# A two-block transformer kernel: nine norms take their inverse root as a square root on ACT and a reciprocal on DVE

## What is computed

```python
def rmsnorm(x, g):
    x32 = x.astype(jnp.float32)
    y = x32 * lax.rsqrt(jnp.mean(x32 * x32, axis=-1, keepdims=True) + EPS)
    return (y * g.astype(jnp.float32)).astype(x.dtype)
...
    x = x + gt1 * (jnp.concatenate([conv_x, attn_x, gla_x], axis=-1) @ w_out)
    x = x + gt2 * swiglu(rmsnorm(x, g2) * (1 + sc2) + sh2, w_up, w_down)
...
        h = rmsnorm_2(x, norm_mix_w[l])
        x = x + hybrid_mixer(h, w_in[l], ...)
        h = rmsnorm_2(x, norm_xattn_w[l])
        x = x + memory_cross_attention(h, mem_n, w_q, w_kv, w_o)
        h = rmsnorm_2(x, norm_ffn_w[l])
        x = x + swiglu_2(h, ...)      # layer 0; a mixture of 8 experts in layer 1
```

## Time and profile before

| | us |
|---|---|
| median of 3 runs | 2685.38 |
| lowest, highest | 2685.04, 2687.94 |
| profiled execution: its own time | 2687.88 |
| profiled execution: its span | 2686.0 |

### The profile page before, as it was taken

How to read it: one execution, slowest core, us unless ns; L and a number is a source line. 1 busy time by engine, 2 the same in 40 slices (tenths; PEclk the granted TensorE clock), 3 DMA queues, 4 the chain that set the end, 5 groups by cost and what they waited for, 6 DMA issues and landing times.

```text
span 2686.0 us, 42788 instructions
## 1 busy us (share of the span) xinstructions
PE 2511.2 (93%) x17242; PEld 2223.3 (83%) x17242; DVE 1757.4 (65%) x2364; ACT 1475.3 (55%) x1888; POOL 27.9 (1%) x85
## 2 busy tenths in 40 slices
PE   4998799999999889999889999897999999999998
PEld 2876579999997689988789998686888888888886
DVE  3445856455455765556555546556888988988887
ACT  3235544444443655455554435554777777777776
POOL 0000000000000000000000001000000000000000
PEclk7998999999999989999999999898999999999999
DMA  7224525445442635445134545231899999999995
GB/s 281 104 100 158 189 95 188 180 182 188 177 160 90 254 136 181 180 159 176 61 126 157 185 177 174 79 136 69 331 358 350 351 357 352 350 356 352 351 356 222
DMA packets 81593, 565.98 MB, mean 211 GB/s; under 512 B 9280, under 2 KB 12608, under 8 KB 13568
## 3 DMA queue, kind: packets, MB, share of 16 engines
q1 hardware_dynamic: 80112, 559.95, 56.1%
q0 software_dynamic: 1296, 3.38, 0.5%
HBM read 559.92 MB, written 1.05 MB: 209 GB/s over the span
## 4 chain that ended last, share of the span: by engine, by line
PE 85%; DVE 8%; ACT 4%; issue 2%; DMA 0%; SPq 0%; DVEq 0%; ACTq 0%
PE psum L232 83%; DVE ring_lo L226 2%; ACT ring_hi L223 1%; DVE hT L739 1%; PE psum L662 1%; PE psum L1880 1%; DVE hT L429 1%; ACT hT L703 1%; DVE hT L1242 1%; ACT Z L711 0%; DMA ring<-in_stream 0%; ACT L415 0%; DVE h_lo L439 0%; DVE Z L1216 0%; DVE Z L1215 0%
## 5 line engine op out<-in xcount | busy, mean ns | idle before, releaser
L226 DVE TENSOR_TENSOR ring_lo<-ring,ring_hi 128x2048 fp32r<-128x2048 f32 x479 | 1096.8, 2291 | 458.5 <-ACT ring_hi L223 455.4
L223 ACT ACTIVATE ring_hi<-ring 128x2048 fp32r<-128x2048 f32 x479 | 916.1, 1914 | 376.9 <-PE psum L232 375.6
L232 PE MATMUL psum<-a_hi,ring_hi 128*128 128x256 f32 (+1 forms) x2448 | 732.7, 299 | 59.8 <-DVE h_lo L437 20.0
L232 PE MATMUL psum<-a_hi,ring_lo 128*128 128x256 f32 (+1 forms) x2448 | 727.3, 297 | 0.0
L232 PE MATMUL psum<-h_lo,ring_hi 128*128 128x256 f32 (+1 forms) x2128 | 629.0, 296 | 0.0
L232 PEld LDWEIGHTS psum<-a_hi,ring_hi 128*128 128x128 f32 x2448 | 476.6, 195 | 78.6 <-issue 43.9
L232 PE MATMUL psum<-ring_hi,a_hi 128*128 128x512 f32 (+1 forms) x1680 | 521.0, 378 | 5.9 <-DVE h_lo L437 3.7
L232 PEld LDWEIGHTS psum<-a_hi,ring_lo 128*128 128x128 f32 x2448 | 476.1, 194 | 10.5
L232 PEld LDWEIGHTS psum<-h_lo,ring_hi 128*128 128x128 f32 x2128 | 414.2, 195 | 7.6
L232 PEld LDWEIGHTS psum<-ring_hi,a_hi 128*128 128x128 f32 x1680 | 313.5, 189 | 58.1 <-issue 4.1
L232 PE MATMUL psum<-ring_lo,a_hi 128*128 128x512 f32 (+1 forms) x976 | 353.2, 362 | 0.0
(11 more groups left out here) (261 smaller groups left out, 2373.5 us busy)
## 6 DMA issues: line engine op xcount, KB each, us to landing
ring<-in_stream SPq DMA_DIRECT2D x529, 1024.0 KB, 4.9
mixT<-mixT POOLq DMA_DIRECT2D x32, 71.0 KB, 5.8
cst<-in_constants SPq DMA_DIRECT2D x1, 1216.0 KB, 15.0
xT<-in_xT SPq DMA_DIRECT2D x1, 1024.0 KB, 9.7
xT<-in_ctxT SPq DMA_DIRECT2D x1, 1024.0 KB, 11.9
xT<-in_memT POOLq DMA_DIRECT2D x1, 1024.0 KB, 6.0
out_y<-hT SPq DMA_DIRECT2D x2, 512.0 KB, 3.1
Z<-in_level_masks SPq DMA_DIRECT2D x1, 448.0 KB, 15.3
```

What stands on the lines that cost most here:

```text
L223: e.activation(hi, raw, ACT.Copy).then_inc(sem("piece_rounded"), 1)
L226: e.tensor_tensor(lo, raw, hi.bitcast(F32), ALU.subtract).then_inc(sem("piece_split"), 1)
L232: ins = pe.matmul(*args, **kw)
```

## The change

`act_rms` computes one function, the square root, and gives its semaphore a new name, `rms`. DVE, which had waited for `inverse_rms`, now calls `dve_invert`: it waits for `rms`, takes the reciprocal in place, waits for its own instruction to finish and goes on. Two preloads name the set of the square root in place of that of the logarithm; the one at the end of the third feed-forward run (`run == 2`), after which `act_two_norms` follows, keeps the logarithm's set.

```diff
@@ -394,7 +394,7 @@
         def act_square_residual(n):
             def step(act, g):
                 if g == 0:
-                    act.preload_act_table_set("natural_log")
+                    act.preload_act_table_set("sqrt_and_others")
@@ -411,8 +411,12 @@
         def act_rms(act, b, n0, n1):
             await_next(act, "mean_square")
             rs = mixT[:, 0, n0:n1]
-            link(act, act.activation(rs, bank[b][:, n0:n1], ACT.Ln, bias=EPS))
-            act.activation(rs, rs, ACT.Exp, scale=-0.5).then_inc(sem("inverse_rms"), 1)
+            act.activation(rs, bank[b][:, n0:n1], ACT.Sqrt, bias=EPS).then_inc(sem("rms"), 1)
+
+        def dve_invert(dve, n0, n1):
+            await_next(dve, "rms")
+            rs = mixT[:, 0, n0:n1]
+            link(dve, dve.reciprocal(rs, rs))
@@ -571,7 +575,7 @@
-            act.preload_act_table_set("natural_log")
+            act.preload_act_table_set("natural_log" if run == 2 else "sqrt_and_others")
@@ -2286,7 +2290,7 @@
                 if layer == 0:
                     dve_first(dve)
-                await_next(dve, "inverse_rms")
+                dve_invert(dve, 0, 2 * T)
```

More of the change, by code:

```diff
@@ L2309, in _ @@
                               at=OUT_BANKS)
-                await_next(dve, "inverse_rms")
+                dve_invert(dve, 0, n)
                 dve_apply(dve, [b1_segment(layer, 1, 0)])
@@ L2325, in _ @@
                 else:
-                    await_next(dve, "inverse_rms")
+                    dve_invert(dve, 0, T)
                     dve_apply(dve, [b2_segment("norm_mix", 1)])
```

## The result

The changed kernel takes 2699.6 us (median of 4 runs, 2699.1 to 2706.0) beside 2685.2 for the kernel before (4 runs, 2684.1 to 2687.9): a ratio of 1.0055 with a 95% interval of 1.0043 to 1.0067. It is 14.4 us slower, where the forecast said 9.8. In the profiled executions the span went from 2686.0 to 2697.7 us, +11.7.

The account below looks back on a forecast made before the run. PE's chain bounds the kernel, and the norms have no cover: 3.5 + 3.2 + 0.7 (norms) + 1.8 (cross-attention loads) + 0.7 (clock) = +9.9 us, giving 2695 us, range 2677 to 2709.

Parts of the forecast that it names:

- a norm has no cover: At each norm, time saved or added between the mean's last matmul and DVE's first multiply passes whole into the time.
- The price of the reciprocal: DVE's reciprocal at the norms: 6.5 ns per element, giving 1.81 us at 256 wide and 3.48 at 512.
- Rival A: Reciprocal at the norms costs like an ordinary elementwise instruction, 1.04 ns per element: -7.5 us, 2678 us; chance 0.17.
- rival C: Reciprocal at the norms takes the lower reading, 5.0 ns per element: +4.5 us, 2690 us; chance 0.13.
- rival B: Reciprocal at the norms takes eight passes per element, 8.3 ns: about +16.4 us, 2702 us; chance 0.20.
- Norm by norm: Cost at the nine norms: norm 1 +3.5 us, norms 2 and 3 +1.6 each, norms 4 to 9 +0.12 each.
- The loads: Five added table loads: about +0.9 us at each of two cross attentions, 0 at the router and two softplus places.
- the sum without the clock: Norms and added table loads together, leaving out PE's half-speed stretches: 9.2 us slower.
- The clock: Longer PE idle at norms 2 and 3 lengthens half-speed work behind them: +0.35 us each, +0.7, bounds 0 to 1.7 each.
- The third rival: From the theory set after the result, not the forecast: the loss beyond the rows is chance of a single trace.
- main case: Reciprocal at the norms costs about 6 to 7.5 ns per element, total 2695 us; chance 0.50.

Follow-up runs that it names:

- twice: Changed kernel with a second reciprocal of the same width, output unread, ahead of the real one at all nine norms: 2720.5 us, ratio 1.0127.
- one_set: Kernel before, with the preloads ahead of eight norms and in the FFN loop naming the set that holds logarithm and exponential: 2673.9 us, ratio 0.9952.
- wide_old: Changed kernel with norms 1 to 3 (512 wide) put back to logarithm and exponential: 2692.9 us, ratio 1.0026 to the kernel before.
- narrow_old: Changed kernel with norms 4 to 9 (256 wide) put back to logarithm and exponential: 2694.7 us, ratio 1.0031 to the kernel before.
- early: Changed kernel with norm 1's reciprocal ahead of the modulation step and the exponential's table loaded earlier before each cross attention: 2689.9 us, ratio 1.0009.
- shift_a: Kernel before with one wide DVE reciprocal into an unread tile added at norm 1: 2690.5 us, ratio 1.0016.
- shift_b: Kernel before with two wide DVE reciprocals into an unread tile added at norm 1: 2695.3 us, ratio 1.0031.
- shift_c: Kernel before with two wide DVE multiplies added at norm 1 as idle work: 2690.8 us, ratio 1.0015.
- one_set_all: As one_set, with the three other preloads (last norm, linear attention's norm, head norm) naming the common set too: 2671.2 us, ratio 0.9943.

## Why the prediction was right, and where it was not

**What bounds the kernel.** That a norm has no cover held at each of the nine: twice shows a second reciprocal whole on the chain, and one_set a removed load whole off it.

**The price of the reciprocal.** Chosen 6.5 ns per element, measured 6.25; 1.81 and 3.48 us against 1.75 and 3.35. The bracket from two-element rows, 5.0 to 8.5, was thin ground that held: the two readings rest on 7 ns between single means, and that the middle of them came within 4% of the measured price was luck. Rival A (ordinary instruction) would have shown 0.42 us at 256, rival C 1.43, rival B 2.28: all three fall by one row. The Trainium skill, "VectorE: DVE Perf Modes", section "Walkthrough: the 8-slice pipeline in each mode", gives the reciprocal a repeat count of 8. Read as eight times the 1.04 ns of an add, as rival B did, that is 8.3 ns. The trace has 6.25, so the count doesn't carry over as a ratio of times.

**Norm by norm.** Norm 1 +3.5 forecast, +3.38 measured; norms 2 and 3 +1.6, measured +1.44; the narrow six +0.12, measured +0.06. The wait of DVE for its own instruction was put at 0.05 us and is 0.03 (383.72 to 383.75).

**The loads.** At the cross attentions +0.9 each, measured 0.96 and 0.97. Router and softplus were put at nothing because waits for PE of 1.73 and 2.25 us cover them, and those waits took them up, down to 0.44 and 0.82. The router's cover is all but used: a load twice as long would show.

So the sum without the clock, 9.2 forecast, is 8.6 by the rows.

**The clock: the term that was mis-sized.** It was +0.7, by 0.35 behind norms 2 and 3, with 3.4 as the upper end. The runs leave 13.6 - 8.6 = 5.0 us beyond the rows (14.4 - 8.6 = 5.8 in the first measurement), more than that upper end; the two traces of the changed kernel give the clock 1.9 to 2.0 us. The step that failed is not only the size. It looked for the loss only at the norms whose idle time grows. At norm 2 it is there, as these stretches show for the kernel after (PE idle, PE at half clock, PE back), beside the earlier trace rows:

```profile
379.70:385.44 5.74, 0.00 (x0) 0.03 (x1) 4.86 (x5) 1.50 (x3) 0.00 (x0) 0.88 0.40 161
385.50:390.50 5.00, 5.00 (x24) 5.00 (x25) 4.82 (x13) 3.34 (x7) 0.00 (x0) 0.50 0.01 3
390.50:394.00 3.50, 3.50 (x29) 3.50 (x29) 0.76 (x2) 2.91 (x2) 0.00 (x0) 0.95 0.00 0
```

5.0 us of work at a granted clock of 0.50, where it was 3.4 us: about 0.8 us lost, a little over the 0.35. At norm 3 the first pair of traces gained a half-clock stretch and the second pair did not. But norm 6, whose idle time grew by only 0.06 us, loses 1.2 to 1.5 us, and other places gain and lose without any edit nearby. What the prediction named last as its risk, a clock that reacts more strongly than two stretches show, is what came; by the rows at norm 6 the length of PE's pauses does not settle how it reacts.

Three things speak for the clock as the main carrier of the remainder. First, the account in the traces: I summed PE's busy time, weighted with one minus the granted clock, from one and the same matmul, that at 70 us, to the end. (Ahead of it the first trace of the kernel before has 5.2 us of this and the others 2.6, without coming later for it.) It is 52.5 and 54.9 us in the two traces of the kernel before and 55.7 in both of the changed one. From that matmul on the changed kernel takes 7.0 and 6.9 us longer than the mean of the two traces before. The rows give 5.2 of it and the clock 2.0 and 1.9, together 7.2. Second, all runs: each lists its span and its mean granted clock. Of 72 runs of the unchanged kernel the 10 with a mean clock of 0.968 or 0.969 have a mean span of 2689.3 us, the 41 with 0.972 or more 2683.6. So the spread of the unchanged kernel goes with the clock too. Third, over the kernels, in the table: "below" is (1 - mean clock) x span of the runs, less that of the kernel before on the same chip. It counts time below full clock in which PE also idles, so it is no price. The last two columns are the account of the first point for each trace, against the mean of the two traces of the kernel before.

| kernel | by the rows, us | measured, us | unexplained | below | unexplained in the trace | clock in the trace |
|---|---|---|---|---|---|---|
| changed kernel | +8.6 | +13.6 | +5.0 | +7.3 | +1.8, +1.7 | +2.0, +1.9 |
| reciprocal twice | +28.0 | +34.7 | +6.7 | +15.7 | +2.5 | +4.8 |
| wide_old | +2.3 | +6.8 | +4.5 | +5.8 | +3.7 | +7.1 |
| narrow_old | +6.3 | +8.6 | +2.3 | +4.2 | 0.0 | +1.3 |
| early | +4.9 | +3.8 | -1.1 | +3.0 | -4.5 | -2.7 |
| shift_a | +3.4 | +4.5 | +1.1 | +2.7 | -3.7 | -3.8 |
| shift_b | +6.6 | +9.3 | +2.7 | +8.2 | +2.6 | +1.6 |
| shift_c | +1.3 | +4.8 | +3.5 | +4.4 | +3.0 | +2.7 |
| one_set | -11.5 | -12.0 | -0.5 | -3.5 | -3.0 | +1.3 |
| one_set_all | -15.4 | -15.0 | +0.4 | -7.4 | -3.9 | -7.0 |

In the changed kernel and the three shift kernels the clock accounts for the trace's remainder to within 1.0 us, in narrow_old to 1.3. In the five others it does not: there PE's idle time, beyond the rows, also moved, by -2.5 us (wide_old), -3.2 (one_set), +3.3 (one_set_all), -2.3 (twice) and -1.2 (early). Of the medians' remainders, those of twice, wide_old and the changed kernel are clear of their intervals, and those of shift_c and early just so. In narrow_old and twice 1.1 and 1.0 us of the measured time lie outside the span, where no row looks. The third rival falls: the changed kernel's loss beyond the rows came in two measurements. The first, that the reciprocal delays other work, does not carry the loss, for beyond the rows PE's idle time behind norm 1 is 0.8 and 0.7 us shorter in the changed kernel's traces, not longer. But such waits do move: from 45 to 290 us the first two traces stay 3.8 to 4.3 us apart, and by 340 us the distance is 1.8, since the first trace of the kernel before lost 2.2 us there to its own second one, in a part where the chain stands mostly with DVE.

Two things stay open. The medians leave 5.0 us beyond the rows where the traces leave 1.8: the traced executions of the kernel before, 2687.9 and 2690.2 us, were slower than its medians, so 3 us of the remainder lie in executions without a trace, for which only the mean clocks speak. And which pause of PE turns into a long half-clock stretch in a given kernel isn't known. The positions can't be set without moving something else, and the table shows that shift_c, the smallest edit, got one of the larger remainders. Why the changed kernel was dearer than early by 9.8 us where rows say 3.75 is answered in kind (in the traces +2.0 against -2.7 us of clock) but not place by place.

**The chances.** Slower by over 0.2% had 0.70, and the interval of 0.43 to 0.67% is there. The main case's number fell short by 4.6 us: the sum without the clock was 0.6 us too high, and what came beyond the rows was more than was allowed for the clock.

## What to carry to other kernels

Price a replacement by its length per element at the width at which it stands on the path, not by the kind of work it is: two short activations without a load between them (0.68 us for 512 wide) beat a square root and a reciprocal (3.41 us), and the load between them went away by naming a set that holds both functions. Before arithmetic is changed to save a table load, see which set each preload names. And where PE pauses often for some microseconds, give a forecast a term as wide as the spread of the unchanged kernel, here 2683 to 2691 us: two edits of 1.3 and 3.4 us on the chain, at a place far ahead, came with changes of +2.7 and -3.8 us in what the half clock cost in their traces.

## What the runs showed of the hardware

- DVE's reciprocal on fp32 took 153 ns + 6.25 ns per element and partition (160 ns at 2, 1753 at 256, 3353 at 512), whether its output is used or not; directly behind another, 3.22 us at 512 in its chain piece. An add of the same shape has 1.04 ns per element.
- A table load took 1283 ns each time; the activation behind it started 0.01 us later, and taking nine of them off the chain gave 12.0 us (9 x 1.28 = 11.5).
- The same code with the same pause of PE, 3.71 us, was followed by 6.4 us at a mean granted clock of 0.73 in one kernel and of 0.52 in another that arrived there 3.9 us later.
